# Norms summed tile by tile beside the last products, and the mixers' side work spread anew, in a two-block transformer kernel on one core

## The reference

```python
# first block, layers 0 and 1
h = h + mixer(rms_norm(h, attn_norm[l]))
h = h + conv_glu_ffn(rms_norm(h, ffn_norm[l]))
# its end
h = rms_norm(h, final_norm)
# second block
h = layer_norm(h, ln_in_g, ln_in_b)
for l in range(2):
    h = layer_norm(DN_ALPHA * h + token_mixers(h), ln1_g[l], ln1_b[l])
    h = layer_norm(DN_ALPHA * h + conv_ffn(h),     ln2_g[l], ln2_b[l])

def token_mixers(h):                      # four branches of 256 channels
    sc_b, sc_c, sc_h, gq, gk, gv, gg, ga_f, ga_b, cq, ckv, kr, cfm_in = split(h @ w_in)
    y_a = sc_b * depthwise_conv(sc_c * sc_h, w_sc_conv)                     # 3 taps
    y_b = rms_norm(gla_scan(forward) + gla_scan(backward)) * silu(gg)       # gated linear attention
    y_c = attention(rope(rms_norm(cq) @ w_uq), rms_norm(ckv) @ w_ukv, rope(kr))
    u   = depthwise_conv(a * sigmoid(gate), w_cfm_dw)                       # 31 taps
    y_d = silu(layer_norm(u))
    return concat(rms_norm(y) for y in (y_a, y_b, y_c, y_d)) @ w_out
def conv_ffn(h):
    g, val = split(depthwise_conv(h @ w_up, w_dw)); return (silu(g) * val) @ w_down
def layer_norm(x, g, b): return (x - mean(x)) * rsqrt(var(x) + 1e-5) * g + b
```

## Time and profile before

| | us |
|---|---|
| median of 3 runs | 2772.95 (2770.27 to 2776.36) |
| the profiled execution | 2777.6 |
| its span, first to last instruction | 2775.8 |
| TensorE, DVE, ScalarE, POOL busy | 2574.1, 1756.5, 1023.1, 975.4 |
| mean granted clock of TensorE | 0.971 |

### The profile page before, as it was taken

How to read it: one execution, slowest core, us unless ns; L and a number is a source line. 1 busy time by engine, 2 the same in 40 slices (tenths; PEclk the granted TensorE clock), 3 DMA queues, 4 the chain that set the end, 5 groups by cost and what they waited for, 6 DMA issues and landing times.

```text
span 2775.8 us, 34461 instructions
## 1 busy us (share of the span) xinstructions
PE 2574.1 (93%) x11354; PEld 1939.0 (70%) x11354; DVE 1756.5 (63%) x2248; ACT 1023.1 (37%) x1608; POOL 975.4 (35%) x389
## 2 busy tenths in 40 slices
PE   8999899999999999999688789999988879899998
PEld 6666688888755688888466366788766646588875
DVE  3755783686376776377597657818638855782772
ACT  3354422232144532232443545313334344532332
POOL 2222344444300044444154033444425403354442
PEclk9999999999999999999899999999999999999999
DMA  4111223232211222222111021222312102122231
GB/s 150 68 43 35 83 94 103 91 101 88 84 46 31 76 91 98 91 98 98 48 64 55 12 77 60 96 93 91 108 62 69 61 15 61 61 101 96 91 100 67
DMA packets 61016, 212.19 MB, mean 76 GB/s; under 512 B 6912, under 2 KB 7168, under 8 KB 60800
## 3 DMA queue, kind: packets, MB, share of 16 engines
q1 hardware_dynamic: 60064, 209.60, 23.0%
q10 hardware_dynamic: 864, 1.44, 0.2%
HBM read 208.92 MB, written 2.10 MB: 76 GB/s over the span
## 4 chain that ended last, share of the span: by engine, by line
PE 69%; DVE 14%; ACT 8%; issue 5%; POOL 2%; DVEq 1%; ACTq 0%; DMA 0%; POOLq 0%; SPq 0%
PE bank_G L518 20%; PE bank_G L520 19%; PE bank_G L519 19%; POOL wlo L452 2%; DVE conv_up L771 2%; ACT whi L491 2%; PE bank_S L570 1%; DVE mx L2369 1%; PE bank_X L1949 1%; DVE prod L791 1%; PE bank_X L840 1%; PE bank_S L1346 1%; PE bank_O L1359 1%; PE bank_O L1593 1%; PE bank_X L1373 1%
## 5 line engine op out<-in xcount | busy, mean ns | idle before, releaser
L452 POOL TENSOR_TENSOR wlo<-raw,whi 128x1024 fp32r<-128x1024 f32 (+2 forms) x367 | 930.6, 2536 | 1701.2 <-ACT whi L491 1701.2
L518 PE MATMUL bank_G<-n_hi,whi 128*128 128x512 f32 x2264 | 917.3, 405 | 50.4 <-DVE n_lo L630 24.0
L520 PE MATMUL bank_G<-n_hi,wlo 128*128 128x512 f32 x2264 | 891.0, 394 | 0.0
L519 PE MATMUL bank_G<-n_lo,whi 128*128 128x512 f32 x2264 | 890.6, 393 | 0.0
L491 ACT ACTIVATE whi<-raw 128x1024 fp32r<-128x1024 f32 (+2 forms) x395 | 410.8, 1040 | 780.8 <-PE bank_G L520 770.9
L518 PEld LDWEIGHTS bank_G<-n_hi,whi 128*128 128x128 f32 x2264 | 430.8, 190 | 179.8 <-issue 52.7
L520 PEld LDWEIGHTS bank_G<-n_hi,wlo 128*128 128x128 f32 x2264 | 430.2, 190 | 93.5
L519 PEld LDWEIGHTS bank_G<-n_lo,whi 128*128 128x128 f32 x2264 | 431.9, 191 | 88.3 <-issue 4.8
L518 PE MATMUL bank_G<-a_hi,whi 128*128 128x512 f32 x704 | 275.3, 391 | 5.6 <-DVE a_lo L793 3.6
L519 PE MATMUL bank_G<-a_lo,whi 128*128 128x512 f32 x704 | 274.0, 389 | 0.0
L520 PE MATMUL bank_G<-a_hi,wlo 128*128 128x512 f32 x704 | 273.9, 389 | 0.0
(11 more groups left out here) (289 smaller groups left out, 2651.2 us busy)
## 6 DMA issues: line engine op xcount, KB each, us to landing
raw<-in_w_mix_in SPq DMA_DIRECT2D x42, 512.0 KB, 3.2
raw<-in_w_hyb_in SPq DMA_DIRECT2D x25, 512.0 KB, 3.2
raw<-in_w_diff_in SPq DMA_DIRECT2D x24, 512.0 KB, 3.2
raw<-in_w_up0a SPq DMA_DIRECT2D x22, 512.0 KB, 3.2
raw<-in_w_up0b SPq DMA_DIRECT2D x22, 512.0 KB, 3.2
raw<-in_w_up1a SPq DMA_DIRECT2D x22, 512.0 KB, 3.2
raw<-in_w_up1b SPq DMA_DIRECT2D x22, 512.0 KB, 3.2
raw<-in_w_up2a SPq DMA_DIRECT2D x22, 512.0 KB, 3.3
```

The source lines that it names most:

```text
L452: pool.tensor_tensor(b.wlo[:, g.slot, 0:width], b.raw[:, g.slot, 0:width], b.whi[:, g.slot, 0:width], ALU.subtract).then_inc(b.lo_ready, 1)
L518: pe.matmul(out, b.whi[:, g.slot, w], hi[:, hi_at + k, :], start=(k == 0), stop=False)
L519: pe.matmul(out, b.whi[:, g.slot, w], lo[:, lo_at + k, :], start=False, stop=False)
L520: mm = pe.matmul(out, b.wlo[:, g.slot, w], hi[:, hi_at + k, :], start=False, stop=(k == pieces - 1))
```

## The change

**Norms.** A class `Norm` describes the five norms (n = 0 to 4; "narrow" behind a mixer, "plain" for n = 0, behind the first block). Beside the products of the last group, tile by tile: after two tiles, the mean of both becomes a shift, which DVE takes off every tile as it comes; ScalarE squares the shifted tiles; DVE adds tiles and squares; TensorE sums with ones into banks O (first moment) and S (second). Behind the last tile the variance is formed from both moments, DVE centres three tiles while ScalarE takes the root, and then scales in place, centres and writes n_lo (now from h and the bias, without waiting for ScalarE's h). For n = 0 the final RMS norm disappears as a stage: ScalarE applies its gain to each tile, squares the plain tile before, and these squares enter the variance with factor EPS2 / D. Loops over tiles in these groups are unrolled.

**Mixers.** Taps are spread otherwise and reach into attention steps 0 to 5; the short convolution works in its own tiles instead of `cpad`; three input tiles instead of two lie in the attention steps; PV moves ahead of the rotations, and these ahead of input tile 17; six copies out of PSUM (VG, VM, the scan's output) move from DVE to ScalarE; the wait for the scan's output moves to the first value product; branches 0 and 1 are swapped and all branch steps are moved; the input columns gg and sc_b are swapped.

```diff
-SUMS_BEFORE = {"HEAD": 0, "MEAN": 1, "BRANCH0": 4, "BRANCH1": 6, "VAR": 7, "BRANCH2": 12}
+SUMS_BEFORE = {"HEAD": 0, "BRANCH0": 5, "MEAN": 5, "BRANCH1": 7, "VAR": 9, "BRANCH2": 15}
-TAPS = (9, 3, 3, 1, 1, 1, 1, 1, 1, 1, 4, 4)
+TAPS = (5, 2, 2, 1, 0, 1, 0, 1, 0, 0, 4, 2, 2, 2, 2, 2, 2, 2)
-LATE_TILES = 19
+LATE_TILES = 18
...
+def norm_tile_pe(pe, b, x, m):
...
+    if m == 2:
+        pe.wait_ge(b.part_ready, x.n + 1)
+        pe.matmul(b.S[:, 0, :], b.k["ones"], b.acc[:, :], start=True, stop=True).then_inc(b.part_summed, 1)
+    if x.narrow and m == 5:
+        pe.wait_ge(b.shift_summed, x.added("q1"))
+        first(b.acc[:, :], True)
+        second(b.mixed[:, 0], True)
+    if x.narrow and m == 6:
+        pe.wait_ge(b.shift_summed, x.added("q3"))
+        second(b.ntmp[:, 0])
+    if m < KD - 1:
+        return
...
+    if x.narrow:
+        pe.wait_ge(b.shift_summed, x.added("q5"))
+        first(b.rstd[:, :])
+        second(b.ntmp[:, 1])
+        pe.wait_ge(b.shifted, 8 * x.n + 7)
+        first(b.h[:, 6, :])
+        pe.wait_ge(b.shift_squared, 8 * x.n + 7)
+        second(b.mixed[:, 1])
+    else:
+        pe.wait_ge(b.shift_summed, x.added("q6"))
+        first(b.acc[:, :], True)
+        second(b.mixed[:, 0], True)
...
+    pe.wait_ge(b.shifted, 8 * x.n + 8)
+    pe.matmul(b.O[:, 0, :], b.k["ones"], b.h[:, 7, :], start=False, stop=True).then_inc(b.first_moment, 1)
+    pe.wait_ge(b.shift_squared, 8 * x.n + 8)
+    pe.matmul(b.S[:, 1, :], b.k["ones"], square_at(b, x, 7), start=False, stop=True).then_inc(b.second_moment, 1)
...
+def norm_tile_act(act, b, x, m):
+
+    split_hi(act, b, Index(x.g0 + m + 2))
...
+    if m == KD - 1:
+        exp_and_ln(act)
+    for k in x.shifts.get(m, ()):
+        act.wait_ge(b.shifted, 8 * x.n + k + 1)
...
+        act.activation(square_at(b, x, k), b.h[:, k, :], ACT.Square).then_inc(b.shift_squared, 1)
...
+def norm_end_dve(dve, b, x):
...
+    variance = dve.scalar_tensor_tensor(b.rstd[:, :], b.S[:, 1, :], 1.0 / D, b.acc[:, :], ALU.mult, ALU.subtract)
...
+    for k in range(AHEAD):
+        centre(k)
+    dve.wait_ge(b.scale_ready, 2 * n + 2)
     for k in range(KD):
...
+        dve.wait_ge(b.centred, 8 * n + k + 1)
+        dve.scalar_tensor_tensor(h[k], h[k], v_(b, x.gain, k), b.rstd[:, :], ALU.mult, ALU.mult).then_inc(b.normed, 1)
+        if k + AHEAD < KD:
+            centre(k + AHEAD)
+        if x.split and k:
+            low(k - 1)
```

In the mixer (DVE's `also` and the order on TensorE):

```diff
+        if step < 6:
+            taps(12 + step)
+        if step == 5:
+            dve.sem_inc(b.cfm_u, 1)
...
-    tile(LATE_TILES - 1)
-
-    taken_out(pe, b, x_at(l, "UQ", 2))
-    rotate_pe(pe, b, Index(g0 + M_KR), x_at(l, "ROT", 0), b.mx[:, M_CKV, :], b.k["rot32"])
...
+    taken_out(pe, b, x_at(l, "UQ", 2))
+    rotate_pe(pe, b, Index(g0 + M_KR), x_at(l, "ROT", 0), b.mx[:, M_CKV, :], b.k["rot32"])
...
+    tile(LATE_TILES - 1)
+
     pe.wait_ge(b.roped, 24 + 2 * (l + 1))
     taken_out(pe, b, x_at(l, "VM", 1))
-    pe.wait_ge(b.g_out, 2 * (l + 1))
```

More of the change, by code:

```diff
@@ L620, in layer_norm_dve @@
[L620 to L639, removed]
+WIDE_ADDS = ("d3", "q1", "q2", "q3", "d4", "q4", "d5", "d6", "q5", "q6")
@@ new lines, with __init__, added @@
+NARROW_ADDS = ("d3", "q1", "q3", "d5", "q5")
+class Norm:
+    def __init__(self, n, group, gain, bias, nhi, split=True):
+        self.n, self.g0, self.gain, self.bias, self.nhi, self.split = n, FIRST[group], gain, bias, nhi, split
+        self.narrow, self.plain = group.startswith("out"), n == 0
+        self.names = NARROW_ADDS if self.narrow else WIDE_ADDS
+        self.before = (n // 2 + n % 2) * len(WIDE_ADDS) + n // 2 * len(NARROW_ADDS)
+        self.shifts = {3: (0, 1, 2), 4: (3, 4)} if self.narrow else {3: (0, 1, 2, 3), 4: (4,)}
+        self.shifts |= {5: (5,), 6: (6,), 7: (7,)}
+    def added(self, name):
+        return self.before + self.names.index(name) + 1
@@ L660, in products_act @@
             split_hi(act, b, Index(g0 + k + 2))
[L661 removed]
+            if k:
                 act.wait_ge(b.evacuated, g0 + k)
                 gained_hi_act(act, b, gain, k - 1)
[L665 to L667 removed]
+        act.wait_ge(b.evacuated, g0 + tiles)
+        gained_hi_act(act, b, gain, tiles - 1)
         return
@@ L674, in products_act, with products_dve @@
     split_hi(act, b, Index(g0 + tiles + 1))
-def products_dve(dve, b, link, name, alpha, stats, gain=None, nhi=0):
+def products_dve(dve, b, name, alpha):
     g0, tiles = group_tiles(name)
[L681 to L692, removed]
-            dve.sem_inc(b.last_ready, 1)
[L694 to L718, removed]
@@ L820, in ffn_dve @@
                    None if first_block else f"dw_up{f - LAYERS}")
-        products_dve(dve, b, link, f"down{f}{tag}", 1.0 if first_block or half else ALPHA, stats if half else None,
-                     gain if half else None, nhi)
+        if half == 0:
+            products_dve(dve, b, f"down{f}{tag}", 1.0 if first_block else ALPHA)
+        elif norm:
+            for m in range(KD):
+                norm_tile_dve(dve, b, norm, m)
+            norm_end_dve(dve, b, norm)
+        else:
+            squared_products_dve(dve, b, link, f"down{f}{tag}", gain, nhi)
 def transpose_pe(pe, b, g, p, src):
@@ L2065, in mixer_pe @@
             mix_out_pe(pe, b, l, "b", m, part)
-    for i, g, g_next in pairs(pe, FIRST[f"out{2 + l}b"] + 2, KD - 2):
-        gemm(pe, b, g, b.n_hi, b.n_lo, KH, None, None, KH, KH)
-        gemm(pe, b, g_next, b.n_hi, b.n_lo, KH, None, None, KH, KH)
+    for m in range(2, KD):
+        mix_out_pe(pe, b, l, "b", m, range(KH))
+        norm_tile_pe(pe, b, NORMS[2 * l + 1], m)
 def mix_out_pe(pe, b, l, half, m, part):
@@ L2190, in also @@
         if step == 3:
+            for j, dst in enumerate((b.rstd, b.mean)):
+                taken_out(act, b, x_at(l, "HEAD", j))
+                act.activation(dst[:, :], dst[:, :], ACT.Exp, scale=-0.5).then_inc(b.head_rs, 1)
+            act.wait_ge(b.evacuated, g0 + M_GG + 2)
+            for j in range(2):
+                act.activation(b.mx[:, M_GG + j, :], b.mx[:, M_GG + j, :], ACT.Silu).then_inc(b.gg_silu, 1)
+            exp_and_ln(act)
+        for n, (squares, take, roots, high) in enumerate(((6, 7, 8, 10), (8, 9, 10, 12), (16, 18, 18, 20))):
+            if step == squares:
+                branch_squares_act(act, b, l, n)
+            if step == take:
+                branch_take_act(act, b, l, n)
+            if step == roots:
+                branch_act(act, b, l, n)
+            if step == high:
+                branch_hi_act(act, b, l, n)
+        if step == 7:
             p = x_at(l, "MEAN")
```

439 lines of the change are left out of this document (263 added, 176 removed).

## The result

The changed kernel takes 2743.22 us in the median of 4 runs (2737.46 to 2745.12), the one before 2773.89 on the same chip: ratio 0.9892, 95% interval 0.9878 to 0.9906. It is faster, by 31 us where I had forecast 69, and 2743 lies above the whole range of 2684 to 2730.

The account below looks back on a forecast made before the run. TensorE, busy for 93% of the span, was taken as the bound, so only its idle or slow-clock stretches could be won. Norms 37.2 plus two mixers 32.0 gave 69.2 us, for a median of 2704 us, range 2684 to 2730.

Parts of the forecast that it names:

- wide norm: Norm behind an FFN: first product ends 22.0 us after the last down product instead of 30.4; gain 6.5 us.
- narrow norms, both: Norms behind the two mixers: 2.8 us gained each, bounds -2 and 5, after charging 3.3; twice 5.6.
- weight split late: Behind a norm, before a mixer: ScalarE's weight split for tile 2 some 0.7 us too late; two mixers, -1.4.
- scan, both: Mixers' scan: shorter waits for score copies and masks, clock partly back; 12.0 us gained a mixer, bounds 7 and 15.
- rope and PV, both: Mixers: rotations moved behind PV products and ahead of one input tile; 3.5 us gained a mixer, bounds 1 and 6.
- attention steps, both: Mixers' attention: taps make VectorE the bound, losing 3; hidden old waits return 3.6; net 0.5 a mixer, bounds -8 and +5.
- (a): Whole kernel: outcome as forecast, own range 2692 to 2718 us; chance 0.60.
- (b): Front of the attention: VectorE bounds it harder, 13 us more a mixer, 2730 us; chance 0.13.
- (c): Product behind four norms: clock stays low through it, 4 x 4.4 us, total 2722; chance 0.07.
- (d): Mixers: every scan wait and half the attention's go, 10 us better a mixer, 2684; chance 0.10.
- (e): Norms: change works only behind the first block, as 24 VectorE operations pace the first product; 2716 us; chance 0.05.
- (f): Attention steps 0 to 5: each tap meets a POOL operation, 53 us a mixer, 2810 us at 24; chance 0.05.

Follow-up runs that it names:

- the sums late: Changed kernel with the three ones products of a narrow norm's partial sums moved from behind tiles 5 and 6 to behind tile 7: 2735.65 us, ratio 0.9891.

## Why the prediction was wrong

Term by term, in us gained:

| term | forecast | measured |
|---|---|---|
| wide norm | 6.5 | 7.6 |
| norm behind the first block | 20.8 | 21.1 |
| last norm | 5.7 | 5.9 |
| narrow norms, both | 5.6 | -3.7 |
| weight split late | -1.4 | in the rows above |
| scan, both | 24.0 | 12.8 |
| rope and PV, both | 7.0 | 7.0 |
| attention steps, both | 1.0 | -21.8 |
| sum | 69.2 | about 29 |

The measured sum and the 6.4 us of clock in unchanged code make the 34.9 between the two spans, within rounding; the medians differ by 30.7.

**Right.** The four norms' length from the last product on, by counting 24 operations on VectorE (16 for the last norm), to within 1 us; that the first pieces come every 1.92 us (1.95 forecast, for all of them); the rope's wait, 3.5 (3.4); the copies' wait in the scan, 2.6 (2.2); and even the new waits in the attention. VectorE's work of steps 0 to 5, forecast at 37.6 us with 5.8 of collisions (its parts make 32.2 and not 31.8, so 38.0), took 36.3 (1499.8 to 1536.1), and TensorE waited 9.9 us where I had 10. Only 6.3 of these were put down to probabilities in steps 5 to 7; 3.6 came in step 3, for the head norm's root. Masks were forecast at a gain of 5.0 of 6.5 and yet with no wait left; 3.6 was left.

**The step that failed: the attention's net of 0.5, bounds -8 and +5.** It measured -10.6 and -11.2. The window over the attention of mixer 0 in the kernel before, to be held against the changed kernel's above:

```profile
1542.42:1620.53 78.11, 66.90 (x261) 39.42 (x261) 46.99 (x100) 48.75 (x93) 9.62 (x7) 0.96 0.08 21
```

TensorE was idle for 11.2 us before. The forecast wrote off all of it, 7.6 as replaced by the new waits and 3.6 as hidden by the moved products, and put 10 of new waits and 0.6 for the later start in its place. The 10 came. But 6.9 of old waits stayed behind step 5: ScalarE's acc 2.5, squares 2.3, the weight split 1.3, pt 0.8, much as in the run without the taps. So the idle time was 16.9, 6.3 more than forecast. In these traces a wait that comes later in the stream was not absorbed by those that came sooner. The other missing term is the clock, for which I had charged nothing here: beyond the 6.0 of the moved work the products took 4.9 more than in the kernel before, and 5.6 more than the same 286 products without the taps (77.8 instead of 72.2). The 6.3 and the 4.9 make the 11.1 by which this term missed, within rounding. The -8 was too near as well: it left out a term, not a spread.

**Narrow norms.** 3.3 was charged for tiles 2 to 7, 8.1 measured (25.5 instead of 17.4 from the start of tile 2 to the last output product). I counted VectorE's five operations at m=4 and left out what is queued ahead of them: residual and three shifts of m=3, slowed by POOL's splits. VectorE in the changed kernel:

```profile
1618.49 0.69 DVE L1702 TENSOR_TENSOR h<-h,bank_G 128x512 f32<-128x512 f32 x1 [2.94 <-PE bank_G L533]
1619.10 2.99 DVE L751 TENSOR_TENSOR h<-h,mean 128x512 f32<-128x512 f32 x3
1622.01 0.68 DVE L1702 TENSOR_TENSOR h<-h,bank_G 128x512 f32<-128x512 f32 x1
1622.60 1.28 DVE L751 TENSOR_TENSOR h<-h,mean 128x512 f32<-128x512 f32 x2
1623.81 1.75 DVE L733 TENSOR_TENSOR acc<-h 128x512 f32<-128x512 f32 x1
1625.48 1.75 DVE L733 TENSOR_TENSOR mixed<-mixed,sq 128x512 f32<-128x512 f32 x1
```

Nine operations without a gap, 8.7 us where nine of 0.69 make 6.2. POOL's splits stood over three of them:

```profile
1619.34 1.59 POOL L465 TENSOR_TENSOR wlo<-raw,whi 128x512 fp32r<-128x512 f32 x1 [2.34 <-ACT whi L504]
1623.43 1.58 POOL L465 TENSOR_TENSOR wlo<-raw,whi 128x512 fp32r<-128x512 f32 x1 [2.50 <-ACT whi L504]
1625.22 1.45 POOL L465 TENSOR_TENSOR wlo<-raw,whi 128x512 fp32r<-128x512 f32 x1 [0.21 <-ACT whi L504]
```

The wait for q1 became 3.3 instead of 1.0, and the ones products and tile 6 behind it ran slowly. TensorE, the wait and the first of the slow products:

```profile
1627.28 1.37 PE L624 MATMUL bank_O<-acc,const 128*128 128x512 f32 x2 [3.29 <-DVE mixed L733]
1628.45 1.92 PE L627 MATMUL bank_S<-mixed,const 128*128 128x512 f32 x2
1629.37 1.42 PE L531 MATMUL bank_G<-n_hi,whi 128*128 128x512 f32 x1
```

That the splits lengthened the queue was read from the timeline and not isolated. With the sums late 4.0 of the 8.1 come back; what stays is close to the 3.3 charged. The Trainium skill (SBUF — State Buffer, Terms) has the loser of the shared port pair fully blocked; two additions of 0.69 that take 1.75 under splits of 1.58 and 1.45 agree with it.

**Scan.** 12.0 forecast, bounds 7 and 15, measured 6.3 and 6.6. The copies gave 4.1 (forecast 4.5), the masks 2.9 (5.0), and the clock cost 0.8 where I had 2.5 coming back. About 2 us of mask waits stay without any tap in the turns, so taps are not the whole of them; that POOL's splits over the decays are the rest (in five of the turns one decay takes 2.0 to 2.6 us, the others 0.41) was read from the timeline and not isolated. The copies' remaining 2.6 is the same with none of the turns' taps and with three taps instead of five or six ahead of turn 0.

**Rivals.** None took the place of (a) as drawn. (b) had the right place and engine, but 13 us a mixer for it would have stood against the rest of the forecast, 2730; the mixers lost 17 each, and the narrow norms 9 more. (c) was put behind four norms; the low clock came behind waits inside the mixers. Against (d), the scan kept 8.8 us of waits a mixer (2.6, 2.6 and 3.6) and the attention's grew; against (e), the wide norm gained 7.6. (f) assumed that each tap meets a POOL operation. The group of taps in steps 0 to 5 of mixer 0, busy time and mean ns of one:

```profile
L2543 DVE SCALAR_TENSOR_TENSOR mx<-cpad,vec,mx 128x512 f32<-128x512 f32 x24 | 19.6, 875 | 1.4 <-DVE mx L2587 0.4 <-DVE mx L2590 0.4 <-DVE mx L2584 0.4
```

That is 0.82 each, where the clear ones take 0.74 and a collision 2.97, so (f) is out.

## What to carry over

Count the queue of the fuller engine through a stretch, and write down as a price of its own what TensorE's products cost behind each new wait: here it was 40% (5.6 of the 14.0 us that the taps cost in the attention). Do not let a new wait replace old ones that lie behind it. Before side work goes beside work that sets the end, look for the longest wait of the engine that does it: 11.8 us ahead of the rope took most of what cost 14 us in the attention. A partial sum that leaves the stream only at the end should be waited for at the end.

## What the hardware did that I had not expected

Without taps in the turns, the same scan with the same waits took 107.5 us in one mixer and 103.1 in the other of one execution, at a granted clock of 0.95 and 1.00; the mixers of the kernel before under the new norms show it too (attention 78.0 at 0.96, 80.8 at 0.92). Behind a longer wait (2.33 instead of 0.93, with 0.97 behind it) eight ones instructions took 6.8 instead of 3.9 us in one mixer and 5.1 in the other. The Trainium skill (TensorE: Matmul & The Clock Gate, What's actually happening) says that how many matmuls run slowly differs between runs of one kernel. The two scans show such a difference inside one run. For a forecast of this kernel it means that a wait of 2.3 to 2.7 us cost between itself (the scan of mixer 1) and itself plus 3, and that the same stretch may differ by 4 us between two mixers with no cause in the code.
